# Second block's mixer: memory side ahead of it, convolution in PSUM between the head norms, attention in pairs of heads

## What is computed

```python
hn = rms_norm(h, mix_norm_g);  proj = hn @ w_in            # q, k, v (8 heads of 64), glu, qm (4 heads of 64)
q, k = partial_rotary(rms_norm(q)), partial_rotary(rms_norm(k))     # per head, before any scaling
attn  = three dilated windows, combined by their log-sum-exp        # S = 256: one softmax with a bias
c  = ga * sigmoid(gg); c = depthwise_conv(c, 31 taps); c = silu(layer_norm(c))
kvm = rms_norm(mem, mem_norm_g) @ w_mem_kv                  # 256 memory rows, 4 heads of 64
mo  = softmax(rms_norm(qm) @ rms_norm(km).T / 8) @ vm
h = h + concat([attn, c, mo]) @ w_out                       # then the feed-forward network
```

## Time and profile before

| what | value |
|---|---|
| median of 3 runs | 1556.16 us |
| profiled execution, its own time | 1552.98 us |
| its span, first to last instruction | 1551.2 us |
| TensorE busy | 1434.7 us (92%) |
| ScalarE, VectorE, GpSimd busy | 688.7, 644.6, 706.7 us |
| mean granted TensorE clock | 0.957 |
| down products of f1 | 1110.6 to 1173.1 us |
| norm, mixer and its output product | 1173.1 to 1349.55 us |
| last norm and feed-forward network | 1349.55 to 1551.2 us |

### The profile page before, as it was taken

One profiled execution on the slowest core, in us unless ns is written; L12 is line 12 of the kernel. 1 busy time (PEld: TensorE's weight loads), 2 busy tenths in 40 slices (PEclk: granted clock), 3 DMA queues, 4 the chain that ended last, 5 costly groups with the idle time before them and its releaser, 6 DMA issues. The chain is left out here.

```text
span 1551.2 us, 24101 instructions
## 1 busy us (share of the span) xinstructions
PE 1434.7 (92%) x8362; PEld 1172.1 (76%) x8362; DVE 644.6 (42%) x1130; ACT 688.7 (44%) x1034; POOL 706.7 (46%) x295
## 2 busy tenths in 40 slices
PE   5899898988899999999989898999999768899998
PEld 1668676866677777788867447899998655799998
DVE  2420772734333333310136633444316977344410
ACT  1552323323434343422257523666646625466642
POOL 0434000432333333344435202688896721478886
PEclk9899999999999999999989879999999978899999
DMA  9422444221545454523224101455565411345564
GB/s 323 132 82 92 180 164 163 82 81 55 180 146 185 143 185 144 180 95 109 96 82 143 55 1 41 149 178 182 181 209 190 156 41 41 109 149 180 185 196 129
DMA packets 60052, 209.95 MB, mean 135 GB/s; under 512 B 6368, under 2 KB 9696, under 8 KB 59872
## 3 DMA queue, kind: packets, MB, share of 16 engines
q1 hardware_dynamic: 59424, 207.39, 39.8%
q10 hardware_dynamic: 576, 1.84, 0.3%
HBM read 208.15 MB, written 1.05 MB: 135 GB/s over the span
## 5 line engine op out<-in xcount | busy, mean ns | idle before, releaser
L237 POOL TENSOR_TENSOR wlo<-raw,whi 128x1024 fp32r<-128x1024 f32 x291 | 706.5, 2438 | 832.2 <-ACT whi L231 832.1
L231 ACT ACTIVATE whi<-raw 128x1024 fp32r<-128x1024 f32 x291 | 306.8, 1055 | 259.9 <-PE ps L251 247.9
L251 PE MATMUL ps<-Hhi,whi 128*128 128x256 f32 (+1 forms) x1368 | 411.8, 325 | 2.5 <-DVE Hlo L1518 1.3
L251 PE MATMUL ps<-Hlo,whi 128*128 128x256 f32 (+1 forms) x1368 | 406.0, 321 | 0.0
L251 PEld LDWEIGHTS ps<-Hhi,whi 128*128 128x128 f32 x1368 | 262.4, 192 | 37.9 <-issue 16.1
L251 PEld LDWEIGHTS ps<-Hlo,whi 128*128 128x128 f32 x1368 | 262.4, 192 | 19.1 <-issue 1.2
L251 PE MATMUL ps<-Hhi,wlo 128*128 128x256 f32 (+1 forms) x1368 | 242.4, 320 | 0.0
L251 PEld LDWEIGHTS ps<-Hhi,wlo 128*128 128x128 f32 x1368 | 204.2, 190 | 18.4
L575 DVE SCALAR_TENSOR_TENSOR u<-ps,par,u 128x255 f32<-128x255 f32 (+1 forms) x132 | 75.4, 572 | 212.5 <-ACT u L539 212.1
L251 PE MATMUL ps<-hidhi,whi 128*128 128x256 f32 (+1 forms) x528 | 155.2, 319 | 0.0
L251 PE MATMUL ps<-hidlo,whi 128*128 128x256 f32 (+1 forms) x528 | 155.1, 319 | 0.0
(11 more groups left out here) (274 smaller groups left out, 1757.4 us busy)
## 6 DMA issues: line engine op xcount, KB each, us to landing
raw<-wstream SPq DMA_DIRECT2D x387, 512.0 KB, 3.3
XT<-x_t SPq DMA_DIRECT2D x1, 1024.0 KB, 10.7
XT<-ctx_t SPq DMA_DIRECT2D x1, 1024.0 KB, 12.8
memx<-mem_t ACTq DMA_DIRECT2D x1, 1024.0 KB, 7.1
out_t<-XT SPq DMA_DIRECT2D x1, 1024.0 KB, 4.8
par<-params SPq DMA_DIRECT2D x1, 457.5 KB, 3.2
glac<-gla_consts SPq DMA_DIRECT2D x1, 384.0 KB, 10.9
mlac<-mla_consts ACTq DMA_DIRECT2D x1, 320.0 KB, 3.5
```

Of the source, the lines that this page charges most:

```text
L231: nc.scalar.activation(whi[:, n % RING, :], raw[:, n % RING, :], ACT.Copy).then_inc(S["hi_ready"], 1)
L237: nc.gpsimd.tensor_tensor(wlo[:, n % RING, :], raw[:, n % RING, :], whi[:, n % RING, :].bitcast(F32), ALU.subtract).then_inc(raw_done[n % ...
L251: mm = nc.tensor.matmul(o, a, b, start=start, stop=stop)
```

## The change

The stages keep their order. Within them:

- Stream: the slots stay where they are in HBM, but are read in another order (QUEUE, SRC): mk, mv, sglu, sqm, q01, k01, q23, k23, sv, so.
- Memory side: memory rows and constants are fetched ahead of the ffn1 norm; squares, totals, root and rows of the memory's norm are computed by ScalarE and VectorE during dn1, through PSUM banks 1 to 3; one product with ones of the totals stands after the second down tile. dn1's TensorE loop is written out. mk and mv are multiplied between the smix sum and the smix rows.
- Rope tables are computed in the head stage; the positions are loaded ahead of the first weights.
- Tiles are made in pairs of 128x512 in one PSUM bank, squared, scaled and rotated from there; the gain is folded into the swap matrix (gsw) and the cosine table, and the root is multiplied on last.
- The convolution accumulates in PSUM bank 6; only its last tap writes to SBUF. Its taps stand in ten pieces between the head norms and rotations.
- Attention runs in six pairs of heads, buffers three deep for the exponentials. The two heads' scores alternate by rows 0 to 63 and 64 to 127 in two banks, their outputs by columns in one bank. GpSimd multiplies by the reciprocals (even_pair), placed in its list between the splits of so; ScalarE writes the high parts of the outputs.
- The output product's first three tiles are done in parts, as pairs become ready.

```diff
@@ stream
+MOVED = [("mk", "mk", 0, 2), ("mv", "mv", 0, 2), ("sglu", "sglu", 0, 4), ("sqm", "sqm", 0, 2),
+         ("sqk", "sqk", 0, 2), ("k01", "sqk", 4, 2), ("q23", "sqk", 2, 2), ("k23", "sqk", 6, 2), ("sv", "sv", 0, 4)]
@@ f1, TensorE
+                for m in range(KD):
+                    down(m % 4, m // 4)
+                    if m == 1:
+                        pe.wait_ge(S["e_tot"], KD)
+                        nc.tensor.matmul(ps[:, 3, 0:T], ones, rstd[:, T:TT], start=True, stop=True).then_inc(S["e_ss"], 1)
@@ f1, VectorE: for one row of the memory's norm
+                nc.vector.scalar_tensor_tensor(x, memx[:, k, :], pc("g_mem", k), ps[:, 3, 0:T], ALU.mult, ALU.mult).then_inc(S["e_xn"], 1)
+                dve.wait_ge(S["e_hi"], k + 1)
+                nc.vector.tensor_tensor(memlo[:, k, :], x, memhi[:, k, :].bitcast(F32), ALU.subtract).then_inc(S["e_lo"], 1)
@@ mixer, VectorE
+                        acc = ps[:, 6, j * T:(j + 1) * T]
...
+                            ins = nc.vector.scalar_tensor_tensor(acc if tap < 30 else cacc[:, j, :], cpad[:, j, tap:tap + T], pc("dw", 2 * tap + j), acc,
+                                                                  ALU.mult, ALU.add)
...
+            conv(0, 5)
+            head_norm("mk")
+            conv(5, 9)
+            head_norm("qm")
+            conv(9, 11)
+            cos_part("q01")
+            conv(11, 16)
+            cos_part("k01")
+            rotate("q01")
+            maxes(0)
+            conv(16, 19)
+            cos_part("q23")
+            rotate("k01")
+            recips(0)
+            conv(19, 23)
+            cos_part("k23")
+            rotate("q23")
+            maxes(1)
+            conv(23, 25)
+            recips(1)
+            rotate("k23")
+            conv(25, 31)
+            maxes(2)
@@ mixer, TensorE
+            for n in range(len(HEADS)):
+                if n == 5:
+                    pe.wait_ge(S["b_exp"], 20)
+                    out_part((0, 1), 0, 4)
+                turns(pe, n)
+                if n + 2 < len(HEADS):
+                    scores(pe, n + 2)
+                if n == 0:
+                    pe.wait_ge(S["s_cv"], 62)
...
+            for qt in range(2):
+                for e in range(2):
+                    r = slice(64 * e, 64 * e + 64)
+                    mm = nc.tensor.matmul(ps[:, SCORE[n][e], qt * T:(qt + 1) * T], sq_[r, tq, qt * P:(qt + 1) * P], sq_[r, tk, :],
+                                          start=True, stop=True)
@@ GpSimd
+        def even_pair(pool, n):
+            pool.wait_ge(S["b_rec"], n + 1)
+            for e in range(2):
+                x = Pb[:, n % 3, e, :, :]
+                nc.gpsimd.tensor_tensor(x, x, brec[:, n % 3, e, :].rearrange("p (q o) -> p q o", o=1).to_broadcast([P, 2, T]),
+                                        ALU.mult).then_inc(S["b_pn"], 1)
```

More of the change, by code:

```diff
@@ L143, in build @@
             Sh = sb(part, "Sh", [P, NCH, 2 * P])
+            posi = sb(part, "posi", [P, T], I32)
         with ExitStack() as part:
@@ L1241, in sums @@
-            def sums(p):
-                pe.wait_ge(S["s_qsq"], p + 1)
-                if p >= 1:
-                    pe.wait_ge(S["s_qlog"], p)
-                nc.tensor.matmul(ps[:, 6, :], blk64, pair(sqs, p), start=True, stop=True).then_inc(S["s_qss"], 1)
-            first_tiles(pe, START["sglu"], (0, 1), xhi, xlo, T, "smix")
-            for a in range(2, 12):
-                tile(a, xhi, xlo)
-                if a == 5:
-                    for k in range(KD):
-                        pe.wait_ge(S["n_msq"], k + 1)
-                        mm = nc.tensor.matmul(ps[:, 7, 0:T], ones, Hf2[:, k, :], start=k == 0, stop=k == KD - 1)
-                    mm.then_inc(S["n_ss"], 1)
-                if a >= 6 and a % 2 == 0:
-                    sums((a - 6) // 2)
@@ L1257, in sec_pe, with pair, sums @@
-            pe.wait_ge(S["secc"], 16)
+            mhi, mlo = (lambda k: memhi[:, k, :]), (lambda k: memlo[:, k, :])
+            def pair(name, slot, hi, lo, between=None):
+                column_tile(pe, slot, SBANK[name], hi, lo, T)
+                if between is not None:
+                    sums(between)
+                column_tile(pe, slot + 1, SBANK[name], hi, lo, T, at=T)
+            def sums(name):
+                i = NORMED.index(name)
+                pe.wait_ge(S["s_sq"], i + 1)
+                if i == 0:
+                    pe.wait_ge(S["s_vm"], 1)
+                else:
+                    pe.wait_ge(S["s_rr"], i)
+                nc.tensor.matmul(ps[:, 7, :], blk64, sqs[:, i % 2, :], start=True, stop=True).then_inc(S["s_ss"], 1)
@@ new lines, in swap @@
+            def swap(name):
+                i = NORMED.index(name)
+                pe.wait_ge(S["s_ev"], i - 1)
+                pe.wait_ge(S["t_gsw"], 2)
+                if i > 2:
+                    pe.wait_ge(S["s_nrm"], i)
+                t0 = TILE0[name]
+                nc.tensor.matmul(ps[:, 5, :], gsw[:, 0 if name[0] == "q" else 1, :], sq_[:, t0:t0 + 2, :].rearrange("p a t -> p (a t)"),
+                                 start=True, stop=True).then_inc(S["s_sw"], 1)
+            pe.wait_ge(S["e_lo"], KD)
@@ new lines, in sec_pe @@
+            pe.wait_ge(*normed("smix"))
+            for j in range(4):
+                column_tile(pe, START["sglu"] + j, (3, 1)[j // 2], xhi, xlo, T, at=T * (j % 2))
+            sums("mk")
+            n = START["sqk"]
+            pair("qm", START["sqm"], xhi, xlo)
+            pe.wait_ge(S["s_nrm"], 1)
+            pair("q01", n, xhi, xlo, "qm")
+            pe.wait_ge(S["s_gg"], 1)
+            pair("k01", n + 2, xhi, xlo, "q01")
+            swap("q01")
+            scores(pe, 0)
+            pe.wait_ge(S["s_nrm"], 2)
@@ L1258, in sec_pe @@
+            pair("q23", n + 4, xhi, xlo, "k01")
+            swap("k01")
+            pe.wait_ge(S["s_xg"], 1)
+            pe.wait_ge(S["s_ev"], 1)
+            pe.wait_ge(S["s_sq"], 3)
+            pair("k23", n + 6, xhi, xlo, "q23")
+            swap("q23")
+            scores(pe, 1)
+            pe.wait_ge(S["s_xg"], 3)
+            pe.wait_ge(S["s_ev"], 3)
+            pe.wait_ge(S["s_sq"], 5)
             for kp in range(4):
@@ L1269, in sec_pe @@
                 if kp == 0:
-                    sums(3)
-            for p in range(4):
-                pe.wait_ge(S["s_qn"], p + 1)
-                pe.wait_ge(S["s_ev"], 9 + p)
-                nc.tensor.matmul(ps[:, p, :], secc[:, 0:P], pair(sq_, p), start=True, stop=True).then_inc(S["s_sw"], 1)
-            tile(12, xhi, xlo)
-            tile(13, xhi, xlo)
-            pe.wait_ge(S["s_glu"], 62)
-            pe.wait_ge(S["n_rv"], NORMS.index("smem") + 1)
-            for j in range(2):
-                mm = nc.tensor.matmul(ps[:, 7, 0:T], ones, cacc[:, j, :], start=j == 0, stop=j == 1)
```

784 lines of the change are left out of this document (454 added, 330 removed).

## The result

The changed kernel took 1506.96 us (median of 4 runs, 1503.95 to 1513.22) against 1556.62 us for the kernel before on the same chip: ratio 0.9685, 95% interval 0.9650 to 0.9719. The profiled execution took 1503.95 us, its span is 1502.0 us; forecast were 1503.6 and 1501.8.

A forecast was written before the change was run, and what follows sets the result against it. TensorE, busy 92% of the span, was taken as the bound, with 36.2 us idle in the second block's mixer. 50.2 - 0.4 - 0.4 = 49.4 us saved gave 1506.8, so 1507 us; range 1496 to 1526.

The forecast's parts named there:

- TensorE's new order: Second block's mixer, TensorE's products laid end to end from 1173.1: sv ends at 1249.1, output product without waits at 1291.2.
- the stretch: From the last down product to the output product's end: forecast 1173.1 to 1299.4, ending 50.2 us earlier than before.
- The convolution in PSUM: Mixer's convolution on VectorE: 62 steps of 0.40 us, free of the stall beside GpSimd, over at 1252.7.
- rival 5: VectorE still stalls beside GpSimd despite PSUM operands; only 20 to 30 us gained, 1526 to 1536; chance 0.03.
- GpSimd's multiplication: Attention's scaling by reciprocals, moved from VectorE: half of 2.4, so 1.2 us each; bounds 0.7 and 2.4.
- rival 4: GpSimd's multiplication with broadcast operand runs far slower than splitting; above 7.3 us each, slower than before; chance 0.02.
- rival 2: Attention's round is longer: GpSimd at 2.4 a multiplication adds 9.6, or clock stays low, +7; 1516 to 1526; chance 0.17.
- The waits of the rounds: TensorE's waits in attention: 1.4 for the convolution, 2.0 ahead of the fifth transposes, 1.8 in small pieces; output product ends 1296.4.
- The clock: Idle and thin work around attention keep TensorE's clock below full; 3 us allowed (0 to 10), end at 1299.4.
- Rival 1: No overlap in the array: each pair of heads costs 2.1 for scores and 2.0 for outputs; +11, 1518; chance 0.10.
- 12.4 the pairing: Attention's scores and outputs: a pair of heads costs what one head cost, 12.4 us over six pairs.
- What costs little: Work outside the mixer: 0.4 us for a product with ones in the down products, 0.4 for early positions, otherwise 0.

The follow-up runs named there:

- Same rows: Changed kernel, but in the scores both heads of a pair take queries and keys from rows 0 to 63; 1503.27 us, ratio 0.9670.
- same columns: Changed kernel with heads taken one after the other and both heads' outputs written to rows 0 to 63 of the bank; 1509.43 us, ratio 0.9708.
- first and third set: Sets of follow-up runs, each repeating the unedited changed kernel beside the kernel before: 1504.29 against 1550.66 us in the first, 1506.44 against 1554.44 in the third.

## Why the prediction was right

- **TensorE's new order.** Right. sv's end was forecast 76.0 us behind the last down product (1173.1 to 1249.1) and came 76.1 behind it (1175.8 to 1251.9). The memory slots fill the norm's gap, and with the gate's slots ahead of them the stretch is 10.6 us longer. TensorE's idle time fell by 29.0 us (36.2 to 7.2), forecast about 30.
- **The convolution in PSUM.** Right, with 0.40 us a step whatever GpSimd does. VectorE's waits between the steps were 12.0 us (forecast 11.6), the convolution ended at 1255.6 (forecast 1252.7, and TensorE was 2.7 late by then), and TensorE waited 1.3 (forecast 1.4). Undone, 17.4 us; rival 5 is out.
- **GpSimd's multiplication.** 1.02 us against my estimate of 1.2, so rival 4 and the first half of rival 2 had no ground; its other half, a low clock through attention, did not come either (0.99 granted over the stretch). The estimate worked out from the Trainium skill's "GPSIMD Engine Reference" (table under "Reconciling with measured numbers"), 1.1 us, was nearer.
- **The waits of the rounds.** Forecast 1.4, 2.0 and 1.8 in pieces, 5.2 in all; measured 1.3, 1.9 and 2.1, 5.3 in all. The sum of the small pieces is partly luck, since they were not named one by one. The reason that I gave for the second (reciprocals behind the layer norm's root) was only half of it: with the reciprocals ahead, the low parts of the outputs are late at the same place. The Trainium skill's rule in "TensorEngine Tiling (Array Packing)", PSUM Bottleneck, is borne out in part: of the 5.2 us that the overlap of the scores saves on TensorE, 2.3 come back as waits for VectorE, ScalarE and GpSimd. Most of these waits are for GpSimd's multiplication and the convolution, not for the evacuation of PSUM itself.
- **The clock.** 3 us were allowed for; the drop in the changed kernel is one of 1.6 us at 1272, so 1.4 of the allowance was not needed. The work behind sv took 0.7 longer than forecast: 49.7 us, less 5.3 of waits and 1.6 of clock, is 42.8 against 42.1. The transposes were quicker there where no wait split them (0.96 to 1.03 a pair for a forecast 1.18), but 1.24 and 1.31, waits not counted, where one did, and mean and variance took 2.0 for 1.7. With 0.1 each for sv's end and the waits that makes 125.8 for 126.3.
- **Rival 1** (no overlap) was priced at 11 us. Same rows and same columns cost 1.1 and 2.1 singly; both at once was not tried, so 11 is not refuted but far from what these two suggest. The price and the sum's line "12.4 the pairing" look like the same error. The overlap saves TensorE 10.3 us of work (0.86 for scores and for outputs, six pairs each), not 12.4, and I booked it in full while the rounds were near the limit of the other engines anyway. The total did not suffer, since the waits had been walked through with the saving in place. What part of the 50 us belongs to pairing, with the operations that it takes off ScalarE and VectorE, stays open, and so does what the tiles of 128x512, the rope tables at the start and the convolution's place between the norms are worth singly.
- **What costs little.** From the second feed-forward norm's product to the mixer's it is 196.4 us before and 196.9 after (980.7 to 1177.6), which fits the 0.4 forecast for the product with ones in the down products. It doesn't prove it: of the twelve later executions ten have 196.9 to 197.0 and two 196.0, and there is one trace of the kernel before. The 0.4 for the positions can't be seen: the first norm's product came at 32.8, before at 33.1.
- **The rest.** Behind the stretch 1.2 us were won that I did not forecast. Right behind the next norm's product the granted clock is 0.93 where it was 0.86:

```profile
1350.90:1375.00 24.10, 22.10 (x161) 0.86 0.38 117
```

```profile
1302.90:1327.00 24.10, 22.13 (x168) 0.93 0.46 149
```

Ahead of the stretch the profiled execution was 2.7 us later than before's (forecast 0.8). The code there is nearly the same and its scatter in later executions is 8 us, so one trace of the kernel before can't tell whether the change costs something there. That trace does pass the earlier norm's product at 366.7, ahead of all thirteen executions of the changed kernel and its variants (366.9 to 374.4). By the medians the gain was 49.7 us in the first measurement and 46.4 and 48.0 in the first and third set, against 49.4 forecast and 52.4 from the stretch and what lies behind it; some 3 to 6 us may be lost ahead of it, and that is open.

- **Luck.** The stretch was forecast within 0.5 us by a walk whose terms came out one by one, and it repeats. That the whole came out within 0.2 us of the forecast (1506.96 for 1506.8) is luck: 1.2 us won behind the stretch and 1.9 lost ahead of it nearly cancel, and medians of the same code differ by more (1504.29 to 1506.96).

## What to carry over

Before an engine is relieved, look in the timeline at what its slow instructions share with their neighbours: here one operand moved to PSUM was worth 17.4 us, three times what moving work between engines brought. Price a saving on the busiest engine in the walk through all engines' lists, not by its count: 5.2 us less of TensorE's work was worth 1 to 2. And put work that depends on nothing into the gap behind a norm, since an idle TensorE is paid twice, once in the gap and once in the lower clock behind it.

## What the runs showed of the hardware

- Products on different halves of the rows or columns overlap in both orders that were tried: a pair's two of one half and then two of the other took 1.07 us (rows) and 1.03 us (columns), alternating ones 1.07 and 1.01, and all four on one half 1.93 and 1.87. The Trainium skill, "TensorEngine Tiling (Array Packing)", Key Properties, says that different tiles can load weights and multiply in parallel; these traces agree.
- More work on TensorE went with a higher clock: with 0.86 us more of products a pair and a longest wait of 1.0 us instead of 1.9 ahead of the fifth transposes, 1271 to 1282 ran at 1.00 instead of 0.84, and 1.6 us came back.
- After 7.2 us of idling TensorE ran at its lower level, 0.50 (1.2 GHz): the first slot of 24 products took 5.14 us instead of 2.87.
- A VectorE operation from SBUF to SBUF stands still beside GpSimd's splitting with two tensor inputs (up to 2.62 us for a step) and, as a TENSOR_SCALAR, with one (2.50 us); with the accumulator in PSUM neither did.
- GpSimd multiplies 128x512 float32 by a broadcast 128x2 in 1.02 us, a little under half of its 2.4 for a subtraction of 128x1024; VectorE needs 0.65 (two in 1.29) if GpSimd is idle.
